# Hybrid decoder block on one core: score buffers, early scores, shares in three products, first expert's rows by tile, reordered loads

## What is computed

```python
proj = rmsnorm(x, norm1_g) @ w_in                       # 512 x 1024 @ 1024 x 3584
o_a = head_rmsnorm(hgrn2(q, f, v), g) * silu(gate)      # 4 heads
o_b = head_rmsnorm(dilated_mixture(q, k, v), g)         # 8 heads
x = x + concat([o_a, o_b]) @ w_out                      # 512 x 1024 @ 1024 x 1024
h2 = rmsnorm(x, norm2_g)
top_vals, top_idx = top_k(h2 @ router_w + router_b, 4)
for each expert e:                                      # 12 MB of weights each
    y = clamped_swiglu(h2[rows of e] @ w_up[e] + b_up[e]) @ w_down[e] + b_down[e]
x = x + gates * y;  return rmsnorm(x, final_norm_g)
```

## Time and profile before

| | |
|---|---|
| median of three runs | 1306.14 us (1304.95 to 1309.43) |
| profiled execution | 1308.46 us, its span 1306.6 us |
| PE busy | 1248.9 us (96%) |
| DVE, ACT, POOL busy | 538.1, 238.5, 135.8 us |
| mean granted PE clock | 0.988 |
| DMA | 450.87 MB, mean 345 GB/s |

### The profile page before, as it was taken

How to read it: one execution, slowest core, us unless ns; L and a number is a source line. 1 busy time by engine, 2 the same in 40 slices (tenths; PEclk the granted TensorE clock), 3 DMA queues, 4 the chain that set the end, 5 groups by cost and what they waited for, 6 DMA issues and landing times.

```text
span 1306.6 us, 33478 instructions
## 1 busy us (share of the span) xinstructions
PE 1248.9 (96%) x14751; PEld 726.3 (56%) x14752; DVE 538.1 (41%) x1045; ACT 238.5 (18%) x485; POOL 135.8 (10%) x144
## 2 busy tenths in 40 slices
PE   6999999999999999999999999999999999999994
PEld 5888876675357565555444455444445454545442
DVE  5767646566424524223242333333333333242424
ACT  6364424421011111010010100010000000010102
POOL 0000001100022221221010101001010101010002
PEclk9999999998999999999999999999999999999997
DMA  9523219027899999999999999999999999999993
GB/s 294 163 65 91 72 45 408 2 114 300 348 395 417 423 415 423 411 415 424 424 424 423 424 424 422 426 422 422 423 424 423 423 424 424 424 423 425 424 390 141
DMA packets 69402, 450.87 MB, mean 345 GB/s; under 512 B 6921, under 2 KB 36077, under 8 KB 44576
## 3 DMA queue, kind: packets, MB, share of 16 engines
q1 hardware_dynamic: 64832, 438.59, 81.5%
q0 software_dynamic: 4416, 10.02, 2.4%
HBM read 441.46 MB, written 9.31 MB: 345 GB/s over the span
## 4 chain that ended last, share of the span: by engine, by line
PE 62%; DMA 32%; DVE 2%; issue 1%; ACT 1%; SPq 0%; DVEq 0%
DMA w_raw_pair<-w_down 29%; PE psum L1945 24%; PE psum L1963 14%; PE psum L1698 8%; PE psum L1695 3%; DMA w_raw_pair<-w_up 3%; PE psum L1974 2%; PE psum L1784 2%; PE psum L1832 1%; PE psum L1808 1%; PE psum L1936 1%; PE psum L1771 1%; PE psum L1849 1%; DMA x_rows<-x 1%; PE psum L2018 1%
## 5 line engine op out<-in xcount | busy, mean ns | idle before, releaser
L1945 PE MATMUL psum<-w_raw_pair,x_slots_turned 128*32 128x512 f32 x4928 | 550.4, 593 | 1.0 <-DMA w_raw_pair<-w_up 0.8
L1945 PEld LDWEIGHTS psum<-w_raw_pair,x_slots_turned 128*32 128x32 f32 x4928 | 208.8, 110 | 280.4 <-issue 218.9
L1963 PE MATMUL psum<-w_raw_pair,a_slots 128*32 128x256 f32 x4992 | 288.3, 380 | 11.7 <-DMA w_raw_pair<-w_down 10.6
L1963 PEld LDWEIGHTS psum<-w_raw_pair,a_slots 128*32 128x32 f32 x4992 | 186.3, 110 | 103.5 <-DMA w_raw_pair<-w_down 15.3
L1522 DVE TENSOR_TENSOR x_rows<-x_rows,psum 128x1024 f32<-128x1024 f32 x106 | 124.6, 1218 | 269.5 <-PE psum L1974 269.5
L845 ACT ACTIVATE lin<-psum 128x768 f32<-128x768 f32 (+1 forms) x32 | 22.5, 704 | 579.3 <-PE psum L1945 579.3
L1491 DVE STREAM_TRANSPOSE a_slots<-glu 128x768 f32<-128x768 f32 (+1 forms) x31 | 26.3, 849 | 202.6 <-PE psum L1963 202.6
L1486 DVE STREAM_TRANSPOSE x_slots_turned<-gathered_quarters 128x256 f32<-128x256 f32 x74 | 43.2, 628 | 113.7 <-PE psum L1945 113.0
L640 POOL COPY gather_quarters<-row_quarters 128x2 int32 (+1 forms) x30 | 16.4, 547 | 691.6 <-DVE x_slots_turned L1486 659.4
L1974 PEld LDWEIGHTS psum<-y_part_group,token_sel 32*128 32x128 f32 x2016 | 63.5, 184 | 42.7 <-issue 42.7
L645 POOL DMA_INDIRECT gathered_quarters<-normed_rows,gather_quarters x74 | 75.0, 1014 | 39.2 <-POOL gather_quarters L640 25.8
(11 more groups left out here) (290 smaller groups left out, 1045.9 us busy)
## 6 DMA issues: line engine op xcount, KB each, us to landing
w_raw_pair<-w_up SPq DMA_DIRECT2D x128, 2048.0 KB, 37.7
w_raw_pair<-w_down SPq DMA_DIRECT2D x64, 2048.0 KB, 37.9
w_in_raw<-w_in SPq DMA_DIRECT2D x28, 512.0 KB, 3.7
w_buf<-w_out SPq DMA_DIRECT2D x4, 1024.0 KB, 8.5
expert_rows<-zero_rows SPq DMA_DIRECT2D x5, 512.0 KB, 6.9
x_rows<-x SPq DMA_DIRECT2D x4, 512.0 KB, 5.2
x_rows<-x SPq DMA_DIRECT2D x1, 2048.0 KB, 17.4
normed_rows<-h_rows SPq DMA_DIRECT2D x4, 512.0 KB, 2.6
```

What stands on the lines that cost most here:

```text
L1945: ins = pe.matmul(U[quarter(j), g, :], slots, up_columns(w, j), start=False, stop=(c == UPC - 1))
L1963: ins = pe.matmul(banks[quarter(j), g, :], slots[:, g, 2 * c + h, :], raw[q.slot(m)][:, at_w:at_w + 256], start=False, stop=(c == DNC - 1 ...
```

## The change

There are three `scores` buffers, by head modulo 3, and maxima and sums for four heads. The scores of heads 0 and 1 stand in the last HGRN head, between its first two value projections, with their maxima and exponentials. Later pairs' scores are split: tiles 0 and 1 in one head, tiles 2 and 3 in the next. A head's transposed probabilities are made one head earlier than its values. Shares begin at the fourth head, column half 0 first; each is 12 fp32r products with gate_T_high, gate_T_low, w_hgrn_high (new, made by ACT) and w_hgrn_low (new, made by POOL, in the free half of w_out_low). Shares 3 and 5 stand behind the last head, share 7 behind the transposes of attn_rows. The first expert's rows are gathered tile by tile, `order` stands behind the first expert's second chunk, `order_experts` on DVE behind the x_slots transposes. SP loads x_rows ahead of w_attn, and the first expert's second and third pair behind share 7, since their buffers hold w_hgrn_high and gate_T_high.

```diff
-        E = over("scores", [P, 2, 1280], fk0)
+        E = [over(f"scores{n}", [P, 1280], (fk0, fk0 + 5120, hg0 + 40960)[n]) for n in range(3)]
+        WGH = over("w_hgrn_high", [P, 2, HH, 512], hg0 + 16384, F32R)
+        GH = over("gate_T_high", [P, HH, SEQ], hg0 + 32768, F32R)
+        GLo = over("gate_T_low", [P, HH, SEQ], g0, F32R)
...
+        SHARED_FROM = 3
+        SHARES = dict(zip(range(SHARED_FROM, AH), share_order))
+        BEFORE_OT, BEHIND_OT = share_order[AH - SHARED_FROM:-1], share_order[-1]
+        W_HGRN_AFTER, W_OUT_AFTER = (0, 0, 1, 2), (3, 4, 5, 6)
+        jobs += pair_scores(-1) + [("pt", 0, c) for c in range(3)]
         for h in range(AH):
-            jobs += [("pt", h, c) for c in range(3)]
             if h in SHARES:
                 jobs += [("xa", SHARES[h])]
-            if h % 2 == 0 and h + 2 < AH:
-                jobs += pair_scores(h + 2)
+            jobs += pair_scores(h)
+            if h + 1 < AH:
+                jobs += [("pt", h + 1, c) for c in range(3)]
             jobs += [("pv", h)]
...
-            for n in range(0, 6, 2):
-                load_pair(FIRST, n, n, 0)
+            load_pair(FIRST, 0, 0, 0)
             sp.wait_ge(S("attn_read"), AH)
             full(sp, "oT", 3)
             sp.dma_start(G2[:, :], norm2_g.to_broadcast([P, D])).then_inc(S("g2_in"), 16)
+            full(sp, "xa", BEHIND_OT)
+            load_pair(FIRST, 2, 2, 0)
+            load_pair(FIRST, 4, 4, 0)
             load_pair(SECOND, 0, 0, 1)
...
+            for h in range(HH):
+                pool.wait_ge(S("g_high"), h + 1)
+                pool.tensor_tensor(GLo[:, h, :], G[:, h, :], GH[:, h, :].bitcast(F32), ALU.subtract).then_inc(S("g_low"), 1)
+            for m in range(4):
+                n, k = m // 2, m % 2 * 2
+                pool.wait_ge(S("w_hgrn_high"), m + 1)
+                pool.tensor_tensor(WOL[:, 0, n, k:k + 2, :], Wb[:, 0, n, k:k + 2, :], WGH[:, n, k:k + 2, :].bitcast(F32),
+                                   ALU.subtract).then_inc(S("w_hgrn_low"), 1)
...
+            probs_turned(0)
+            for h in range(HH):
+                freed(act, "gT", h)
+                act.activation(GH[:, h, :], G[:, h, :], ACT.Copy).then_inc(S("g_high"), 1)
+            for h in range(AH):
+                if h + 1 < AH:
+                    probs_turned(h + 1)
+                if h + 2 < AH:
+                    exps(h + 2)
+                for m in range(4):
...
+            masked_max(2, (0, 1))
+            probs_turned(0)
+            masked_max(3, (0, 1))
...
+                if heads:
+                    masked_max(heads[0], tiles)
+                if h + 1 < AH:
+                    probs_turned(h + 1)
+                if heads:
+                    masked_max(heads[1], tiles)
...
+                if i == TT - 1:
+                    dve.wait_ge(S("slot_rank_in"), 16)
+                    dve.wait_ge(S("placed"), TT - 2)
+                    slots_of((0, 1))
                 add_share("x2", i, 1)
...
-                for k in range(HH):
-                    ins = pe.matmul(o, G[:, k, i * P:(i + 1) * P], Wb[:, 0, n % 2, k, :], start=(k == 0), stop=(k == HH - 1))
+                for first, rows, w_rows in ((True, GH, WGH[:, half, :, :]), (False, GH, WOL[:, 0, half, :, :]),
+                                            (False, GLo, WGH[:, half, :, :])):
+                    for k in range(HH):
+                        ins = pe.matmul(o, rows[:, k, i * P:(i + 1) * P], w_rows[:, k, :], start=(first and k == 0),
+                                        stop=(rows is GLo and k == HH - 1))
...
             rows_turned(TT - 1, 1)
+            first_rows(0)
             logits(TT - 1)
+            first_rows(1)
             places(TT - 2)
             places(TT - 1)
+            first_rows(TT - 2)
+            first_rows(TT - 1).then_inc(t_full, 1)
...
-            order()
+            freed(pe, "pos")
+            freed(pe, "x2", TT - 1, 1)
             up_bias(0, groups(0))
             pe.wait_ge(t_free, X0 + 1)
             for c in range(UPC):
                 up_chunk(FIRST, c, groups(0), True)
                 if c == 0:
                     next_rows()
+                if c == 1:
+                    order()
```

225 lines of the change are left out of this document (122 added, 103 removed).

## The result

| | before | after |
|---|---|---|
| median | 1307.12 us (4 runs, 1304.95 to 1309.43) | 1290.91 us (4 runs, 1290.17 to 1292.87) |
| ratio to before | | 0.9873, 95% interval 0.986 to 0.9886 |
| profiled execution, its span | 1308.46, 1306.6 us | 1290.17, 1288.4 us |
| mean granted PE clock | 0.988 | 0.994 |

The time fell by 16.2 us in the medians, by 18.3 in the two profiled executions. The prediction was 1290.6. As will be seen, this close agreement is partly luck: the sum of 15.5 us was some 3 us short of what the traces show.

A forecast was written before the change was run, and what follows sets the result against it. The prediction took the end as a full DMA stream whose start PE sets. Terms 12.7 + 3.5 - 0.8 = 15.4, say 15.5 us, off the 1306.1 us median gave 1290.6; range 1284 to 1299.

The forecast's parts named there:

- The frame: From about 354 us the end is a full DMA stream; PE sets its start, which could move up to 19 us.
- Part 1: Scores of heads 0 and 1 and their exponentials inside the last HGRN head: 2.4 us of products leave the attention.
- t0: The moment the attention begins, predicted as 190.8 + 3.0 = 193.8 us.
- Part 2: First three heads without shares, bound by ACT: 15.7 us of PE work in 18.9 before the first share.
- Part 3: Shares in three products from the fourth head: 0.71 us less each, 36.9 us from first share to attn_rows transposes.
- rival 1: First three heads slower: three attn_sq held up by POOL, up to 7.1 us; 1296 with 5.5 of it; 24%.
- The clock: PE's granted clock in the attention: one stretch at 0.50 expected, costing 2 us.
- Part 4: First expert's rows gathered tile by tile, two tiles moved up around the last logits: 3.5 us saved.
- Order: Order's three products move behind chunk 1, where nothing hides them: 0.8 us lost before the gates of 330 us and later.
- Part 5: Two of the first expert's pairs load behind the last share, x_rows before w_attn: both costed at nothing.
- Rival 2: No fall of the clock in either place, attention or first expert's rows: 2 us and 1.6 us more, 1287; 12%.
- Rivals 3, 4 and 5: Loads cost 9.9 us, 1300.5 (5%); three products not shorter, 1296.3 (3%); PE stays at clock 0.50 through attention, 1327.5 (2%).

The follow-up runs named there:

- fp32 shares: The changed kernel with shares as four fp32 products again, without the ACT copies and POOL differences made for them; 1293.56 us, ratio 0.9906.
- scores late: The changed kernel with scores, maxima and exponentials of heads 0 and 1 behind the HGRN part again; 1289.39 us, ratio 0.9867.
- rows late: The changed kernel with the first expert's rows of all four tiles together again behind the choice; 1294.98 us, ratio 0.9911.
- order first: The changed kernel with order's three products ahead of the first expert again, DVE's part ahead of them; 1291.53 us, ratio 0.9856.

## Why the prediction was right, and where it was not

**The frame held.** The end follows the gate one for one: 975.5 to 977.7 us from there to the end in all kernels, 976.4 before. The stream could move by 19 us, and did. Since the whole gain lies ahead of the gate, it can be laid out on it: 18.96 us, between one trace of either kernel. The three of the changed kernel have the gate at 310.96 to 311.21; the kernel before has one.

**Part 1 and t0.** Predicted 193.8, measured 194.2; what the early scores add to HGRN was right in size. That early scores are worth having was half wrong: they move 2.5 us and win 0.9 at most.

**Part 2.** The first share was to start 18.9 us behind t0, it started 18.0 behind (212.13). That PE waits for ACT here was right: 0.4 us were won by the early table, 0.3 by two copies moved behind it. What binds is the sequence through the table load, as the forecast had it, and not the copies made beside it (fp32 shares). The "2.7 us gap" in the third head was 1.0.

**Part 3.** A share was to take 2.73 us and takes 2.80; from the first share to attn_rows 36.9 us were forecast and 38.4 measured. Of the 1.5 more, 0.5 is the shares' length, and 0.7 is what PE's wait for x_rows was worth, behind a DVE that attn_sq held up: rival 1's mechanism. The forecast's "all other engines under PE" was wrong there. The waits of 4.5 us behind the maxima went, as forecast. Undoing the three products costs 4.82 us, against 5.7.

**The clock** is the first step that failed: "I expect one such stretch at about the same price, 2 us". There was none, in either place. Parts 1 to 3 gave 269.01 - 255.04 = 14.0 us instead of 12.7: 2.0 more by the clock, 0.7 less by the rest (t0 later by 0.4, part 3 longer by 1.5, part 2 shorter by 0.9, the steps behind attn_rows shorter by 0.2). The place in the first heads is settled only as far as this: with one wait of 1.0 us the clock stayed at 1.00, and so it did with waits of 1.0 and 0.8 us (scores late); with one of 2.25 (first share in the third head) it fell to 0.61 in that window, and before, with one of 1.8, to 0.50.

**Part 4** is the second: 3.5 us forecast; from the first w_out product to the first expert 43.4 us against 49.3, so 5.9. The tiles alone are worth 4.25 with the clock that they save. The remaining 1.7 is mostly the last logits: I held them at 3.2 us, which was their length at the slow clock, and they took 1.92. So I had priced the clock's fall on the rows only (1.6 us) and not on the logits that it had also slowed (1.3 us). Why they run at full clock now is open: with the rows late the gap of 0.78 us ahead of them is back, and they take 1.94 all the same. The clock was still 1.00 from 288.6 to 290.6 us there and fell behind them, to 0.50 from 291 on; before, it was 0.50 from 303 to 304, in the middle of them. With one trace of each, these 1.3 us may be a matter of the execution and not of the change.

**Order.** -0.8 forecast; the first chunk moved by 19.9 us and the gate by 18.96, so -0.9. That nothing is lost against the old place is new: there DVE would be late. 14.0 + 5.9 - 0.9 = 19.0.

**Part 5.** Nothing, as forecast, for the first expert's pairs. The new place of the x_rows load was not undone by itself.

**The rivals.** Rival 2 (no fall of the clock, 12%) is what happened; its 3.6 us on top of 15.5 give 19.1, and the gate moved by 18.96. That these agree so well is luck too: parts 1 to 3 gave 0.7 less than its 14.7, part 4 0.8 more than its 5.1. The forecast at 52% had the right parts and the wrong clock. Its number, 1290.6, is a gain of 15.5 taken from a median of 1306.1. Four runs of the kernel before gave 1307.12, and the first four of the changed kernel were among its slowest (1290.91, later 1288.42 and 1289.56); the gains against the kernel before, measured beside each, were 16.2, 18.8 and 17.5 us. Rival 1's mechanism is real, and its sign came true: DVE is on the chain in the first heads, and attn_sq was held in two of the three heads named (in the first it met no POOL operation). But its price was 0.7 us, not up to 7.1: DVE had slack, as was argued against it. Rivals 3, 4 and 5 did not come.

**The parts together.** Undone one at a time, the three products cost 4.8, the tiles 4.25, early scores 0.9: 10 of 19.9 us ahead of the order's loss. The rest was not undone as one piece: it would be the third buffer and the empty first heads, with the waits of 4.5 and 1.8 us and the stretched scores (1.7) that they removed, 8.0 together, and the logits' 1.3. That they add up to 19.3 fits less well than it looks, since other waits changed too: PE's 1.5 us for attn_rows and 1.2 for attn_T_high are gone, and 1.0 for scores and 0.4 for x_rows are new. This last part is argued from rows, not shown by a run: no run has the changed kernel with the old two buffers.

## What to carry to other kernels

Filling a gap of PE can pay twice where the clock falls behind it; when pricing that, count every instruction of the slow stretch at its full-clock length, not only those that are moved. When the end is a DMA stream of fixed size, measure changes from a fixed point of the program to the first buffer gate; here that distance repeated to 0.02 us while medians moved by 2.5. Before work goes to POOL, look for DVE operations with both inputs in SBUF on the chain beside it, small ones too, and give one input from PSUM or put them off; here that was worth 0.7 us. Before work is taken from an engine that others wait for, see whether the wait is for its amount or for one sequence through it: ACT without 2.2 us of copies kept PE waiting just as long.

## Of the hardware, not expected

- A DVE product of 128x4 elements with both inputs in SBUF took 2.29 us beside a POOL operation of 2.38 us, and 0.16 without.
- The hold goes both ways: a POOL operation that started together with a DVE one took 1.33 us and not 1.04, and DVE's kept its 0.42.
- Three fp32r products were cheaper here than one fp32 product of the same size: 12 records in 2.80 us against 8 in 3.49 us for a share.
- In one trace (order first) the clock was 0.60 over 4 us behind waits of 0.94 and 0.72 us with small products between them; in the changed kernel waits of 1.0, 0.6 and 0.7 us left it at 1.00.
- From the o_rows transposes to the gate, 117.6 us in which four engines and SP's queue hand over to each other, five traces agree to 0.02 us; the scatter of the total time comes from before and behind.
